# Second mixer: the scans' inputs pass through SBUF, copied by ScalarE, and VectorE multiplies them in operations of 128x512

## The reference

```python
bu_re = jnp.einsum('bsgh,gph->bsgp', uf, bb_re)
bu_im = jnp.einsum('bsgh,gph->bsgp', uf, bb_im)
_, _, st_re, st_im = lax.associative_scan(_complex_affine_combine, (ar, ai, bu_re, bu_im), axis=1)
y = (jnp.einsum('bsgp,ghp->bsgh', st_re, c_re) - jnp.einsum('bsgp,ghp->bsgh', st_im, c_im) + d_skip * uf)
y = jax.nn.gelu(y.reshape(bsz, s, D_SSM))
y = y * jax.nn.sigmoid(jnp.einsum('bsc,ce->bse', y, w_glu) + b_glu)
```

## Time and profile before

| what | us |
|---|---|
| median of 3 runs | 1300.24 (1299.71 to 1301.41) |
| the profiled execution, its time | 1303.72 |
| its span, first to last instruction | 1301.8 |
| TensorE busy | 1269.5 (98%) |
| VectorE busy | 998.9 (77%) |
| ScalarE busy | 604.3 (46%) |

### The profile page before, as it was taken

One profiled execution on the slowest core, in us unless ns is written; L12 is line 12 of the kernel. 1 busy time (PEld: TensorE's weight loads), 2 busy tenths in 40 slices (PEclk: granted clock), 3 DMA queues, 4 the chain that ended last, 5 costly groups with the idle time before them and its releaser, 6 DMA issues.

```text
span 1301.8 us, 25351 instructions
## 1 busy us (share of the span) xinstructions
PE 1269.5 (98%) x10727; PEld 1224.3 (94%) x10727; DVE 998.9 (77%) x1595; ACT 604.3 (46%) x864; POOL 88.8 (7%) x159
## 2 busy tenths in 40 slices
PE   8899999999999999999999999999999998999998
PEld 7899999999999999999999989999999987999997
DVE  3799998877888667999988877899966757655554
ACT  3543334566433636333345755333354566533333
POOL 0111110000011040111110000000001000000000
PEclk8999999999999999999999999999998999999999
DMA  9899998441888652999993425555523522444551
GB/s 369 352 382 376 360 355 313 138 154 35 319 341 306 244 197 114 359 362 353 352 383 116 162 82 193 196 191 196 211 85 115 195 65 82 178 179 179 193 195 49
DMA packets 66096, 293.83 MB, mean 226 GB/s; under 512 B 7744, under 2 KB 8896, under 8 KB 51904
## 3 DMA queue, kind: packets, MB, share of 16 engines
q1 hardware_dynamic: 47552, 225.10, 47.4%
q0 software_dynamic: 18432, 67.12, 12.9%
HBM read 291.14 MB, written 1.05 MB: 224 GB/s over the span
## 4 chain that ended last, share of the span: by engine, by line
PE 88%; DVE 6%; ACT 3%; issue 1%; DMA 1%; SPq 0%; DVEq 0%; ACTq 0%
PE gu_bank L611 16%; PE gu_bank L609 16%; PE gu_bank L610 16%; PE y_bank L609 7%; PE y_bank L610 7%; PE y_bank L611 7%; PE t_bank L609 2%; PE t_bank L610 2%; PE t_bank L611 2%; PE gu_bank L661 1%; PE gu_bank L662 1%; PE gu_bank L665 1%; DVE dn_lo L1738 1%; PE y_bank L635 1%; DVE rstdT L1687 1%
## 5 line engine op out<-in xcount | busy, mean ns | idle before, releaser
L609 PE MATMUL gu_bank<-hT_hi,gu_hi 128*128 128x256 f32 x1668 | 463.5, 278 | 3.5 <-DVE gu_lo L1752 1.7
L611 PE MATMUL gu_bank<-hT_hi,gu_lo 128*128 128x256 f32 x1668 | 463.3, 278 | 0.0
L610 PE MATMUL gu_bank<-hT_lo,gu_hi 128*128 128x256 f32 x1668 | 463.1, 278 | 0.0
L609 PEld LDWEIGHTS gu_bank<-hT_hi,gu_hi 128*128 128x128 f32 x1668 | 314.6, 189 | 5.1 <-issue 2.3
L610 PEld LDWEIGHTS gu_bank<-hT_lo,gu_hi 128*128 128x128 f32 x1668 | 314.8, 189 | 0.8
L611 PEld LDWEIGHTS gu_bank<-hT_hi,gu_lo 128*128 128x128 f32 x1668 | 314.7, 189 | 0.0
L1298 ACT ACTIVATE sg<-gu_bank 128x256 f32<-128x256 f32 x110 | 42.3, 385 | 495.2 <-PE gu_bank L611 495.2
L1743 DVE TENSOR_TENSOR gu_lo<-raw_gu,gu_hi 128x2048 fp32r<-128x2048 f32 x105 | 240.8, 2293 | 37.0 <-ACT gu_hi L1285 31.9
L1285 ACT ACTIVATE gu_hi<-raw_gu 128x2048 fp32r<-128x2048 f32 x100 | 191.1, 1911 | 14.5 <-DMA raw_gu<-ffn_gu 14.5
L1637 DVE SCALAR_TENSOR_TENSOR stage<-stage,c_row 128x1024 f32<-128x1024 f32 x128 | 150.6, 1220 | 0.0
L609 PE MATMUL y_bank<-act_hi,dn_hi 128*128 128x256 f32 x528 | 146.4, 277 | 2.0 <-DVE act_lo L1778 2.0
(11 more groups left out here) (473 smaller groups left out, 2238.5 us busy)
## 6 DMA issues: line engine op xcount, KB each, us to landing
raw_gu<-ffn_gu SPq DMA_DIRECT2D x110, 1024.0 KB, 6.3
stage<-ada POOLq DMA_DIRECT2D x128, 512.0 KB, 7.8
raw_dn<-ffn_dn SPq DMA_DIRECT2D x110, 512.0 KB, 3.7
ring<-mix_w SPq DMA_DIRECT2D x72, 512.0 KB, 3.6
stage<-ada SPq DMA_DIRECT2D x8, 512.0 KB, 14.7
pro<-ada SPq DMA_DIRECT2D x6, 512.0 KB, 13.9
x<-x_in SPq DMA_DIRECT2D x1, 1024.0 KB, 5.5
ring<-ada SPq DMA_DIRECT2D x2, 512.0 KB, 17.7
```

What stands on the lines that cost most here:

```text
L609: pe.matmul(to, a[0], b[0], start=start, stop=False)
L610: pe.matmul(to, a[0], b[1], start=False, stop=False)
L611: return pe.matmul(to, a[1], b[0], start=False, stop=stop)
```

## The change

ScalarE copies each scan's inputs out of the four banks into `bu_sb`, two buffers in `hT[:, 4:8]`, which is free at that time, with four copies of 128 partitions by 2 x 64 for each scan. A new semaphore `bu_out` counts them. VectorE waits for its scan's four copies and then makes the first turn with two products of 128x512 instead of eight of 128x128. The copies for scans 0 and 1 stand at the start of step n = 5 of ScalarE's loop, those for scan 2 at the start of n = 8, those for scan 3 at the start of n = 10; the last two also wait until the buffer has been read. `glu` on TensorE, which writes into two of the banks, waits for the copies instead of the products.

```diff
@@ names @@
+        bu_sb = hT[:, 4:8, :].rearrange("p (u r) s -> p u r s", u=2)
@@ TensorE, glu @@
-                    pe.wait_ge(bu_used, 8 * UT)
+                    pe.wait_ge(bu_out, 4 * UT)
@@ ScalarE @@
+            def states_in(u):
+                act.wait_ge(bu_ps, 1)
+                if u >= 2:
+                    act.wait_ge(bu_used, 2 * (u - 1))
+                for s in range(4):
+                    act.activation(bu_sb[:, u % 2, :, MT * s:MT * (s + 1)], yb[s][:, P * u:P * (u + 1)].rearrange("p (r n) -> p r n", r=2), ACT.Copy).then_inc(bu_out, 1)
+
             for n in range(12):
                 if n in (9, 10):
                     gelu(n - 9)
+                if n == 5:
+                    states_in(0)
+                    states_in(1)
+                if n in (8, 10):
+                    states_in(n // 2 - 2)
                 act.wait_ge(tile_ps, base + n + 1)
@@ VectorE, scan @@
-                dve.wait_ge(bu_ps, 1)
-                for s in range(4):
-                    bu = yb[s][:, P * u:P * (u + 1)].rearrange("p (r n) -> p r n", r=2)
-                    for to, table in ((ma, ecos), (mb, esin)):
-                        dve.tensor_tensor(to[:, :, MT * s:MT * (s + 1)], bu, table[:, 4 * u + s, :].unsqueeze(1).to_broadcast([P, 2, MT]), ALU.mult).then_inc(bu_used, 1)
-                dve.wait_ge(bu_used, 8 * (u + 1))
+                dve.wait_ge(bu_out, 4 * (u + 1))
+                for to, table in ((ma, ecos), (mb, esin)):
+                    turn = table[:, 4 * u:4 * u + 4, :].rearrange("p s m -> p (s m)").unsqueeze(1).to_broadcast([P, 2, S])
+                    dve.tensor_tensor(to[:, :, :], bu_sb[:, u % 2, :, :], turn, ALU.mult).then_inc(bu_used, 1)
+                dve.wait_ge(bu_used, 2 * (u + 1))
```

More of the change, by code:

```diff
@@ L302, in program @@
             sem("lift_ready"), sem("win_ps"), sem("win_out"), sem("near_zero"), sem("near_ps"), sem("near_out"), sem("near_done"), sem("u_out"))
-        bu_ps, bu_used, states_done, c_ps, v_used = sem("bu_ps"), sem("bu_used"), sem("states_done"), sem("c_ps"), sem("v_used")
+        bu_out, bu_ps, bu_used, states_done, c_ps, v_used = sem("bu_out"), sem("bu_ps"), sem("bu_used"), sem("states_done"), sem("c_ps"), sem("v_used")
         gelu_done, glu_ps, sig_done, glu_done, sq2_done, ssm_ss, ssm_rooted, mix2_done = (
```

## The result

| | before | after |
|---|---|---|
| median of the runs, us | 1300.61 (10 runs, 1298.92 to 1303.33) | 1306.85 (10 runs, 1303.43 to 1310.73) |
| ratio, 95% interval | | 1.0044 (1.0033 to 1.0056) |
| the profiled execution, its span | 1303.72, 1301.8 | 1305.71, 1303.8 |

The change makes the kernel slower, by 6.2 us between the medians; 1306.3 was forecast, 6.1 more than before. The two profiled executions differ by 2.0 us only. Executions of one and the same kernel differ by some microseconds, so the profile is read within the stretch, from the end of the scans' inputs on, not by its end.

What follows compares the result with a forecast made beforehand. TensorE, busy 98% of the span, was taken as the bound. Products 0, copies' busy time 0 and their late place 6.1 us, added to the 1300.24 us median, gave 1306.3 us, range 1304.2 to 1308.6.

Steps and rivals of the forecast that it cites:

- Where the copies stand: ScalarE's queue: copies behind unit 8's split wait for tile 5, so VectorE starts scan 0 7.4 us late.
- The copies' size: ScalarE: 0.26 us a copy, overlapping by 0.1; four last 0.75 us, eight 1.4 us.
- The products: VectorE's scans: two wide products for eight save 0.38 us a scan, worth 0 because hidden under TensorE.
- Tile 8, 4.4 us late: TensorE: tile 8 starts at about 1015.75 instead of 1011.36, waiting for unit 8's low half; idle 4.0 us.
- The late start of scan 0: VectorE: released at 1007.85 instead of 1000.42, 7.4 us late.
- The clock: TensorE after the idle time: clock at half for 3.4 us, losing 1.7 us.
- rival 1: TensorE's clock at half for 6.8 us, loss 3.4 instead of 1.7; tile 9 7.8 us late, 1308.0 us; chance 0.14.
- It fills the wait for unit 9 and does not add to it: TensorE before tile 9: the 1.7 us clock loss falls inside a 1.6 us wait; tile 9 about 6.1 us late.
- TensorE does not wait for VectorE there: Stretch 1000 to 1030 us: TensorE busy all 30 us, so shorter VectorE products are worth 0.
- rival 4: Faster: VectorE's shorter scans bring low halves and TensorE's tiles forward; -1.5 us, 1298.7; chance 0.03.
- The range: Spread around the forecast time, 1304.2 to 1308.6 us, with 0.3 us of spread on each side.
- rival 2: Stall taken back behind tile 11, or TensorE's wait ends sooner: 4.4 us only, 1304.6; chance 0.05.

Runs made afterwards that it cites:

- experiment 1: Changed kernel with the copies for scans 0 and 1 moved ahead of the split of unit 8; 1.0002 against the kernel before.
- Experiment 2: Kernel before, without copies, plus a VectorE wait ahead of scan 0 until ScalarE has split unit 8; 1.0051, 1308.18 beside 1302.05 us.
- experiment 6: Changed kernel with 14 matmuls of zeros on TensorE ahead of tile 8's wait for unit 8; 1.0047 against the kernel before.
- experiment 5: Changed kernel with only scan 0's copies moved ahead of the split of unit 8; 1.0004 against the kernel before.
- experiment 4: Changed kernel with early copies, and eight products of 128x128 out of the copies instead of two of 128x512; 1.0003 against the kernel before.
- experiment 8: Changed kernel with early copies, and the four skip-weight operations on VectorE ahead of scan 0; 0.9998 against the kernel before.
- experiment 10: Changed kernel with early copies and the gate's weights loaded later, skip weights where they were; 0.9993 against the kernel before.
- experiment 11: Changed kernel with early copies, skip weights ahead of scan 0 and the gate's weights loaded later, run once more; 0.999, 1298.09 beside 1299.72 us.
- experiment 7: Kernel before, with the gate's weights loaded after the scans' inputs, behind the loads of units 8 to 10; 0.9991 against the kernel before.
- experiment 3: Changed kernel with the copies for scans 0 and 1 one step later, behind the split of unit 9; 1.0069, 1310.64 beside 1302.05 us.

## Why the prediction was right

- **Where the copies stand** decides: shown from both sides, by taking the place away and keeping the copies (1.0002) and by keeping the wait without the copies (1.0051). Of the four sets scan 0's makes the loss (1.0004 with only this one early).
- **The copies' size.** 0.75 us for four and 1.4 for eight was forecast; four take 0.76 and eight 1.47 in the trace. One copy takes 0.296 us on average, not 0.26, and they overlap by 0.13, not 0.1: two small misses that cancel.
- **The products.** 0.38 us less a scan was forecast; measured from the first product to `vin` 1.33 instead of 1.71. Forecast to be worth 0 in the time; measured 1.0002 for the wide and 1.0003 for the narrow form, equal within 2.4 us.
- **Tile 8, 4.4 us late.** TensorE waited 3.99 us before it and 0.15 before tile 7, as forecast. Counted from the inputs' end, though, tile 8 starts at 14.2 instead of 11.0 us, 3.2 late. The late start of scan 0, forecast as 7.4 us behind the inputs' end, was 1004.09 - 997.88 = 6.2 in the profile, because tile 5, for which the split waits, took 1.2 us less under a shorter spell of half clock. That term hangs on the clock, which I had not said; with the spell of before it would be about 7.4.
- **The clock**, 1.7 us for the shorter spell: in the profile it was the longer one, 2.7 us (rival 1's mechanism, to which I gave 0.14). Since the earlier spell was shorter by as much as this one was longer, the sum came out near the forecast in this profile, 5.8 us; that is luck. Against experiment 1's profile, whose earlier spell is the same 3.4 us, tile 9 is 6.3 us late, counted from the inputs' end: 1019.72 - 997.88 = 21.84 here and 1014.40 - 998.86 = 15.54 there. Which spells the other executions had is not recorded, so how the 6.2 us of the medians divide between wait and clock stays open. Experiment 2 shows the case as forecast: a short spell and then 0.18 us of waiting for unit 9.
- **"It fills the wait for unit 9 and does not add to it"** holds for the short spell only: experiment 2 has 0.18 us of waiting left behind it. With the clock at full, in experiment 6, the wait appears, 1.22 us where 1.6 was worked out. The long spell of the changed kernel's profile used it up and added 1.1 us.
- **"TensorE does not wait for VectorE there"** was too strong. In the profile of before, unit 9's low half is done at about 1015.7 and tile 9 starts at 1016.47, a margin of 0.8 us, and it stands on a tile 5 at half clock. With the copies early, TensorE waits for this low half 0.37, 0.74 and 0.94 us in the profiles of experiments 5, 4 and 8. This is a part of rival 4, too small to show in any ratio.
- **The range.** 1304.2 to 1308.6 leaves 0.4 us under rival 2's 1304.6 and 0.6 over rival 1's 1308.0, not the 0.3 on each side that I wrote.

## What to carry to other kernels

Before work is moved to an idle engine, look at what the instruction ahead of it in that engine's list waits for. ScalarE was idle for 12 us in front of the very place, and the copies inherited that whole wait, since they stood behind it; ahead of that split they cost nothing that could be measured. And price a later start on an engine by the margin of what is queued behind it (here 2.7 us, in front of unit 8's low half), not by that engine's share of busy time.

## What the runs showed that I had not expected

TensorE's clock fell to its half (1.2 GHz) behind the scans' inputs in most profiles, for 3.4 us (after) or 6.8 us (before), and in three (experiments 8, 10 and 11) not at all; the gap was 1.3 us in before, after and experiment 8 alike. No kernel was profiled twice. But the 29 runs of before beside experiment 7 have mean granted clocks from 0.987 to 0.995 and times from 1298.01 to 1304.35 us, the lowest clock in the longest run, so executions of the same kernel seem to differ by such spells, and single profiles of two kernels can't be compared by their spans: 2.0 us between the spans here, 6.2 us between the medians.

The gap without a releaser in a row of 256 small matmuls depends on the loads beside it: 0.93 to 2.19 us in nine profiles with the gate's weights under way (0.93 in experiment 2, 2.19 in experiment 3), 0.41 us in experiment 7, 0.60 in experiment 11 and none in experiment 10 with them moved.
